# Five edits in a fused two-block transformer kernel: two earlier table loads, a later prefetch, a spreading stage that ends without waiting for its stores, and fewer score tiles beside it

## The reference, cut to what matters

```python
def rms_norm(x, g):
    y = xf * lax.rsqrt(jnp.mean(xf * xf, axis=-1, keepdims=True) + NORM_EPS)
    return (y * g).astype(x.dtype)

ml = (sc @ mod_w[i] + mod_b[i]).reshape(bsz, 1, N_MOD, d)      # modulation rows
hl = hl + ml[:, :, 5] * _peer_ffn(xl, pr_w_q[i], pr_keys[i], pr_u[i], pr_v[i])
hc = hc + mc[5] * _peer_ffn(xc, ...)                           # even layer only

# _peer_ffn: 8 heads choose 16 of 16384 rows for each token
a = jnp.einsum('nd,nhkd->nhk', xt, u[eidx])
w = gate * jax.nn.gelu(a, approximate=False)
return jnp.einsum('nhk,nhkd->nd', w, v[eidx])
```

## Time and profile before

| | us |
|---|---|
| median of 3 runs (3866.75 to 3868.51) | 3867.3 |
| the profiled execution's own time | 3863.82 |
| its span | 3862.0 |
| PE busy in the span | 3638.1 (94%) |
| PE weight loads | 3236.8 (84%) |
| DVE busy | 2690.2 (70%) |
| ACT busy | 1704.9 (44%) |
| POOL busy | 711.8 (18%) |

### The profile page before, as it was taken

How to read it: one execution, slowest core, us unless ns; L and a number is a source line. 1 busy time by engine, 2 the same in 40 slices (tenths; PEclk the granted TensorE clock), 3 DMA queues, 4 the chain that set the end, 5 groups by cost and what they waited for, 6 DMA issues and landing times. The chain is left out here.

```text
span 3862.0 us, 59455 instructions
## 1 busy us (share of the span) xinstructions
PE 3638.1 (94%) x22541; PEld 3236.8 (84%) x22541; DVE 2690.2 (70%) x5241; ACT 1704.9 (44%) x2738; POOL 711.8 (18%) x672
## 2 busy tenths in 40 slices
PE   8997999989999896999999999999988899999998
PEld 7895888878878776888899999999976888888887
DVE  5664666556665758887878868888566887777776
ACT  4454445445543544454222332223235554555554
POOL 0001000000010104554444313333010660000000
PEclk9998999999999998999999999999989999999999
DMA  6555655565542123346888868888421366556664
GB/s 250 190 203 213 246 189 214 186 231 201 186 143 103 47 77 120 121 167 259 304 316 302 317 222 312 306 307 313 176 94 61 132 239 234 214 212 213 213 223 164
DMA packets 166486, 793.72 MB, mean 206 GB/s; under 512 B 16608, under 2 KB 58176, under 8 KB 96992
## 3 DMA queue, kind: packets, MB, share of 16 engines
q1 hardware_dynamic: 120208, 603.88, 42.9%
q0 software_dynamic: 45744, 186.36, 13.5%
q10 hardware_dynamic: 288, 0.15, 0.0%
HBM read 743.04 MB, written 47.28 MB: 205 GB/s over the span
## 5 line engine op out<-in xcount | busy, mean ns | idle before, releaser
L247 DVE TENSOR_TENSOR units<-ring,units 128x1024 fp32r<-128x1024 f32 x857 | 1048.5, 1225 | 561.7 <-ACT units L240 558.2
L240 ACT ACTIVATE units<-ring 128x1024 fp32r<-128x1024 f32 x922 | 972.3, 1056 | 1009.0 <-PE ps L277 838.0
L276 PE MATMUL ps<-units,weighted 128*128 128x512 f32 x1280 | 501.3, 392 | 0.0
L275 PE MATMUL ps<-units,weighted 128*128 128x512 f32 x1280 | 499.4, 390 | 1.1 <-DVE units L247 1.1
L277 PE MATMUL ps<-units,weighted 128*128 128x512 f32 x1280 | 500.2, 391 | 0.0
L275 PE MATMUL ps<-wide_four,units 128*128 128x384 f32 (+1 forms) x1208 | 396.7, 328 | 8.7 <-PEq L3725 8.7
L277 PE MATMUL ps<-wide_four,units 128*128 128x384 f32 (+1 forms) x1208 | 394.9, 327 | 0.0
L276 PE MATMUL ps<-wide_four,units 128*128 128x384 f32 (+1 forms) x1208 | 394.4, 326 | 0.0
L277 PEld LDWEIGHTS ps<-units,weighted 128*128 128x128 f32 x1280 | 240.3, 188 | 51.2
L275 PEld LDWEIGHTS ps<-units,weighted 128*128 128x128 f32 x1280 | 240.9, 188 | 46.2 <-DVE units L247 1.5
L276 PEld LDWEIGHTS ps<-units,weighted 128*128 128x128 f32 x1280 | 240.7, 188 | 43.7
(11 more groups left out here) (592 smaller groups left out, 8141.1 us busy)
## 6 DMA issues: line engine op xcount, KB each, us to landing
ring<-in_stream SPq DMA_DIRECT2D x469, 1024.0 KB
quad_ring<-in_mod_w POOLq DMA_DIRECT2D x12, 4096.0 KB, 14.6
gates_dram<-gates_place SPq DMA_DIRECT2D x20, 2048.0 KB
gates_place<-gates_dram SPq DMA_DIRECT2D x16, 1536.0 KB
gates_place<-gates_dram SPq DMA_DIRECT2D x16, 1024.0 KB
gain_rows<-in_norm_gains SPq DMA_DIRECT2D x6, 512.0 KB, 4.4
peer_keys<-in_keys SPq DMA_DIRECT2D x3, 1024.0 KB, 6.3
ml_mask<-in_ml_mask SPq DMA_DIRECT2D x1, 2048.0 KB, 7.9
```

The lines of the kernel that those rows point to most:

```text
L240: act.activation(K.parts(n)[0], K.raw(n), ACT.Copy).then_inc(K.sig("hi_made").sem, units_to(K, n))
L247: dve.tensor_tensor(lo, K.raw(n), hi.bitcast(FP32), ALU.subtract).then_inc(K.sig("unit_split").sem, units_to(K, n))
L275: pe.matmul(out, w[0], x[0], start=start, stop=False)
L276: pe.matmul(out, w[0], x[1], start=False, stop=False)
```

## The change

The Sqrt table is asked for by a Sqrt of one element, in the opening ahead of the wait for x and in the odd layer's head ahead of the squares. There ACT now also copies the context tile out of PSUM, and DVE multiplies it by its row later, between the two norms. GpSimd's load of quad 0 comes after its other work and after 12 units are used. Five tiles are made beside each spreading (9 and 7 before), so 13 and 15 experts have their activations ahead, and the stream's order of units and the plan of picks follow. In spreading ACT evacuates everything before it splits the next two units, and the block ends without a wait for the stores. A part of each block is copied straight to where the first chunk of gates is read (SBUF to SBUF, beside the store), the first chunk is not loaded from DRAM, and the waits for the stores stand in the expert stage, on DVE ahead of the first gates and on SP ahead of chunk 1.

```diff
--- before.py
+++ after.py
@@ -61,8 +61,8 @@
 FFN_SLOTS = FT + FT // 2
 PEER_SLOTS = PEER_HEADS + KEYS
 
-AHEAD = 7, 7, 3
-AHEAD_BOTH = 5, 9, 3
+AHEAD = 7, 5, 3
+AHEAD_BOTH = 5, 5, 3
 
 
 TRIO = 3 * P
@@ -889,8 +889,11 @@
         self.picked_sum, self.loads = picked_sum, loads
 
     def scalar(self, act):
-        prepare_scalar(self.K, act, self.lat)
-        high_parts(self.K, act, self.lat, range(KD))
+        K, other = self.K, self.other
+        act.activation(other.y[:, 0, :], product(K, MT), ACT.Copy).then_inc(other.made.sem, 1)
+        act.activation(K.stat[:, 59:60], K.stat[:, 59:60], ACT.Sqrt)
+        prepare_scalar(K, act, self.lat)
+        high_parts(K, act, self.lat, range(KD))
 
     def between_scalar(self, act, c):
         if c == 0:
@@ -901,13 +904,12 @@
             high_parts(self.K, act, self.ctx, range(4 * c - 4, 4 * c))
 
     def vector(self, dve):
-        K, S, other = self.K, self.mine, self.other
+        K, S = self.K, self.mine
         dve.wait_ge(*S.loaded)
         for t in range(MT):
             dve.tensor_tensor(S.y[:, t, :], product(K, t), S.row, ALU.mult).then_inc(S.made.sem, 1)
             dve.wait_ge(*S.made.at(t + 1))
             dve.tensor_tensor(self.lat.src[:, t, :], S.res[t], S.y[:, t, :], ALU.add).then_inc(S.summed.sem, 1)
-        dve.tensor_tensor(other.y[:, 0, :], product(K, MT), other.row, ALU.mult).then_inc(other.made.sem, 1)
         prepare_vector(K, dve, self.lat)
         whole_columns(K, dve, self.lat, range(KD))
 
@@ -916,6 +918,8 @@
             K, S = self.K, self.other
             dve.wait_ge(*S.loaded)
             dve.tensor_tensor(S.y[:, 1, :], self.picked_sum, S.row, ALU.mult).then_inc(S.made.sem, 1)
+            dve.wait_ge(*S.made.at(1))
+            K.orders["dve"](dve, dve.tensor_tensor(S.y[:, 0, :], S.y[:, 0, :], S.row, ALU.mult))
             add_products(K, dve, S)
             prepare_vector(K, dve, self.ctx)
 
@@ -1645,11 +1649,12 @@
 
             @block.gpsimd
             def _(pool):
-                if opening is not None:
-                    load_quad(K, pool, 0)
                 entry_gpsimd(K, pool, entry)
                 if ahead is not None:
                     ahead.gpsimd(pool)
+                if opening is not None:
+                    pool.wait_ge(K.sig("unit_used").sem, 12)
+                    load_quad(K, pool, 0)
 
             @block.tensor
             def _(pe):
@@ -3790,18 +3796,18 @@
                         while taken < beside.count and beside.last_group(taken) < n - 1:
                             beside.scalar(act, taken)
                             taken += 1
+                while stores < groups // 2:
+                    store(stores)
+                    stores += 1
                 while taken < beside.count:
                     beside.scalar(act, taken)
                     taken += 1
                 for unit in beside.next_units():
                     split_hi(K, act, unit)
-                while stores < groups // 2:
-                    store(stores)
-                    stores += 1
     iota_made.past(1), iota_moved.past(1)
     by_act.past(groups // BUFFERS), by_pool.past(groups - groups // BUFFERS)
     compared.past(groups), spread.past(groups), stored.past(groups // 2)
-    beside.past(), keep.past()
+    beside.past()
 
 
 def u_unit(e, ahead):
@@ -3835,19 +3841,18 @@
     def before(self, act, t):
         g = t // SPAN
         if t % SPAN == 0 and g >= 2:
-            act.wait_ge(*self.moved[g % 2].at(16 * (g // 2)))
+            act.wait_ge(*self.moved[g % 2].at(32 * (g // 2)))
 
     def sync(self, sp, stored, tokens, also):
         for g in range(self.spans):
             also((g + 1) * SPAN)
             sp.wait_ge(*stored.at((g + 1) * SPAN // tokens))
+            sp.dma_start(self.chunks[0][:, g, :, :], self.blocks[g % 2][:, 0:CHUNK, :]).then_inc(self.moved[g % 2].sem, 16)
             sp.dma_start(self.dram[g], self.blocks[g % 2]).then_inc(self.moved[g % 2].sem, 16)
+
+    def wait_moved(self, eng):
         for n in range(2):
-            sp.wait_ge(*self.moved[n].at(16 * self.spans // 2))
-
-    def past(self):
-        for n in range(2):
-            self.moved[n].past(16 * self.spans // 2)
+            eng.wait_ge(*self.moved[n].at(16 * self.spans))
 
     def load(self, sp, c):
         sp.dma_start(self.chunks[c % 2].rearrange("p g e n -> p g (e n)"),
@@ -3855,16 +3860,18 @@
           .then_inc(self.moved[c % 2].sem, 16)
 
     def wait_loaded(self, eng, e):
-        if e % CHUNK == 0:
-            c = e // CHUNK
-            eng.wait_ge(*self.moved[c % 2].at(16 * (c // 2 + 1)))
+        c = e // CHUNK
+        if e == 0:
+            self.wait_moved(eng)
+        elif e % CHUNK == 0:
+            eng.wait_ge(*self.moved[c % 2].at(16 * self.spans + 16 * ((c + 1) // 2)))
 
     def gates(self, e):
         return self.chunks[e // CHUNK % 2][:, :, e % CHUNK, :]
 
-    def past_loads(self):
+    def past(self):
         for n in range(2):
-            self.moved[n].past(16 * KEYS // CHUNK // 2)
+            self.moved[n].past(16 * self.spans + 16 * (KEYS // CHUNK // 2 - 1 + n))
 
 
 GATHERS = 4
@@ -3952,8 +3959,9 @@
         with K.block() as block:
             @block.sync
             def _(sp):
-                for c in range(2):
-                    store.load(sp, c)
+                stream_weights(K, sp, u_unit(A, A) // 2)
+                store.wait_moved(sp)
+                store.load(sp, 1)
                 for c in range(2, KEYS // CHUNK):
                     done = CHUNK * (c - 1) - 1
                     stream_weights(K, sp, v_unit(done, A) // 2)
@@ -4104,7 +4112,7 @@
                     split_ahead(K, dve, split_lo, K.taken + KEYS)
     K.taken += KEYS
     early_taken.past(A - N), gelu_done.past(KEYS - A), weights_made.past(STEPS * KEYS)
-    store.past_loads()
+    store.past()
     if joint:
         lows_copied.past(KEYS - A), summed.past(KEYS - A)
     if picked is not None:
```

## The result

The changed kernel takes 3841.1 us, the median of 4 runs (3840.60 to 3849.32); the kernel before took 3867.8 in the same comparison (4 runs, 3866.75 to 3868.51). The ratio is 0.9937 [0.9924, 0.9949]: 26.7 us faster, where 3.7 were forecast, and outside the range. A second measurement of the same kernel gave 3842.9 (5 runs) against 3865.9 (24 runs), ratio 0.9938 [0.9925, 0.9952], 23.0 us.

The account below looks back on a forecast made before the run. PE was taken to bound the expert stretches, waiting for others only in the opening, the first spreading and the ends of spreading. Terms -2.8 - 5.4 + 0 - 8.6 + 22.3 - 8.2 - 1.2 + 0.2 = -3.7 gave median 3863.6 us, range 3856.5 to 3871.5.

Parts of the forecast that it names:

- my first term: First spreading, 9 to 5 tiles: DVE's waits for PE fall from 8.7 to 1.1 us; with restarts, 8.6 us gained.
- Opening, start: Opening, ahead of the first norm: two table loads leave ACT's path and x comes 0.4 earlier; 2.8 us gained.
- Stall: Opening, steps 1 to 4: ACT's wait for ring slot 3 and the slow PE behind it go; 5.4 us gained.
- Tiles' new place: Expert loops: six tiles move into the main part, four at 4.18 and two at 2.80 us; cost 22.3 us.
- Gaps: Ends of both spreadings: PE's wait falls from 8.7 and 8.8 to 4.6 us, 4.1 gained each, 8.2 in all.
- Clock after the gap: Behind both ends of spreading: PE loses 1.6 us to the slow clock, a gain of 0.6 each, 1.2 together.
- D: Rival: the gap is short enough for the fast clock to stay; 3860.4, or 3859.3 with x earlier; chance 0.15.
- Odd head: Odd layer's head: PE comes 1.1 us earlier and its unit 0.3 later; cost 0.2 us.
- B: Rival: the ring starves anyway in the opening, so the 5.4 us are lost; 3869.0; chance 0.12.
- C: Rival: the first spreading doesn't shrink, as a score piece still delays the compares; 3872.2, slower by 4.9; chance 0.10.
- F: Rival: the changed tiles do nothing because the pieces were free; excluded beforehand by 33 waits, given no chance.
- E: Rival: a table switch holds ACT longer than its record, so 3.8 us more would go; 3859.8; chance 0.08.

Follow-up runs that it names:

- The three single experiments: Kernel before with one part of the change each: the opening alone, ratio 0.9973; the tiles alone, 0.9987; the end of spreading alone, 0.9976.
- the two single edits: Kernel before with only the early Sqrt in the opening, 3864.84 us, and with only the later load of quad 0, 3859.50 us; one execution each.

## Why the prediction was wrong

**The step that failed** is the price of the spreadings. I divided a run of 118 compares without an idle row by 117, got 0.646 us, and took that for what DVE can do; from it came "The second stage, 7 to 5 tiles, has nothing to give but these 1.1: I take 0", and a first stage that could lose only its 8.7 us of shown waits with their restarts. DVE's own rate is 0.598: with three tiles all but a few steps at the start have it, and fewer tiles don't lower it. The 0.646 was a mean of two kinds of steps. The rows of the kernel before in narrow windows of the timeline, two pairs of compares out of that very run, then one pair of the even layer:

```profile
3110.55 1.41 DVE L3751 TENSOR_TENSOR hits<-ps,routes 128x512 f32<-128x512 f32 x2
3111.27 1.29 DVE L3751 TENSOR_TENSOR hits<-ps,routes 128x512 f32<-128x512 f32 x2
```

```profile
1680.84 1.47 DVE L3751 TENSOR_TENSOR hits<-ps,routes 128x512 f32<-128x512 f32 x2
```

A compare's record lasts 0.68 to 0.69 us, so two that follow at DVE's rate fill 1.28 or 1.29 together. The pair of 1.41 stands 0.72 apart, the pair of 1.47 0.78, the latter with 0.10 us of idle time between its two records. Neither is shown as a wait. Two things hide it: at full rate a record ends 0.68 - 0.598 = 0.08 us after the next compare could have begun, and a row of the timeline also takes in compares with a little idle time between them, 0.10 us here. What the late one waits for stands in the timeline of PE, same kernel:

```profile
3110.62 0.61 PE L3765 MATMUL ps<-hits 128*128 128x128 f32 x4
```

PE is through with a group at 3111.23, and the late compare starts at 3111.27. This holds throughout. In the even layer of the kernel before, 74 of 191 steps are over 0.62 us, in the odd one 49 of 127, and each of these compares starts 0.036 to 0.039 us after the end of PE's work on the group five before, the one whose buffer it takes (PE's ends are modelled, but the distance is always the same). Only 33 and 3 of them show a wait.

| time above 0.598 a step, us | even, before | even, change | odd, before | odd, change |
|---|---|---|---|---|
| late compares with a shown wait | 11.4 (33) | 1.6 (3) | 1.4 (3) | 0 |
| late compares without one | 7.5 (41) | 0.2 (2) | 5.4 (46) | 0.5 (3) |
| all other steps | 0.7 | 0.0 | 0.5 | 0.0 |
| together | 19.6 | 1.9 | 7.2 | 0.5 |

The difference is 17.7 us in the first stage and 6.7 in the second, as the spreadings measured. So the late compares without a shown wait, which I had at nothing, are 7.2 of the 9.1 us that my first term missed and 4.9 of the 6.7 of the second. The restarts, 0.08 us each and not 0.034, are 1.2 more in the first; the three shown waits with theirs are 1.4 in the second; 0.7 and 0.4 are steps of 0.61 in place of 0.60. Together 15.8 were missing, and the other terms take 0.5 of it back. The Trainium skill, Perfetto Trace Analysis, section Optimizing Scalar/DVE Operations, says that of the fixed time of each DVE instruction the half that acknowledges the write overlaps with the next one, so that the profiled latency is longer than the engine is busy; these rows agree in that, with 0.68 against 0.598.

The sign was to be had from the kernel before. Its first seven compares, where the first score piece of PE is still ahead (1660.23):

```profile
1654.37 4.28 DVE L3751 TENSOR_TENSOR hits<-ps,routes 128x512 f32<-128x512 f32 x7
```

(4.28 - 0.68) / 6 = 0.600 us, far below the 0.646 that I took for the rate. I had asked of such runs only whether a wait is shown.

With this the sum is: -7.0 for the opening, -17.7 and +16.9 for the even tiles, -6.7 and +5.6 for the odd ones, -5.1 and -5.2 for the two ends, +0.2 for the odd head, in all -19.0 us. The three single experiments give by their ratios -10.4, -5.0 and -9.3, together -24.7, each within some 4 us; the change as a whole -24 [-29, -19] in the second measurement. So the parts agree with the whole, as far as such intervals can tell: the -19.0 of the rows lies just inside that interval (and just outside the one of the first measurement, -29 to -20). The rest, 4 us against the second median and 8 against the first, is not settled. In the two profiled executions it is not one more stage of the change, since all stretches behind the first compare are accounted for to 2 us; the faster executions, which make the median, have no profile. In the first measurement the granted clock was 0.978 in the profiled execution and 0.980, 0.981 and 0.980 in the other three; 0.002 of 3841 us is, as an estimate, 8 us of full clock, and by 8 us they were shorter. In the second the order isn't that plain (3842.69 us at 0.978, 3843.57 at 0.980).

That the tiles cost 22.5 us, as forecast, and gave back 24.4 means that this edit by rows is worth 1.9 us. The gain of the change is that of the opening and of the two ends.

**The scatter** lies in code that the change doesn't touch, and goes at least partly with PE's clock. The kernel with the tiles alone is the kernel before up to the spreading, and reached its first compare at 1660.71 in place of 1654.37. Timeline of GpSimd, the kernel before and then the one with the tiles alone:

```profile
1105.91 2.43 POOL L571 TENSOR_TENSOR both_pair<-whole_columns,both_pair 128x256 fp32r<-128x256 f32 x2 [6.44 <-DVE whole_columns L564]
...
1451.44 0.14 POOL L3396 IOTA peer_iota<- 128x16 f32 x1 [133.35 <-POOLq L1345]
```

```profile
1105.70 2.43 POOL L571 TENSOR_TENSOR both_pair<-whole_columns,both_pair 128x256 fp32r<-128x256 f32 x2 [6.43 <-DVE whole_columns L564]
...
1457.59 0.14 POOL L3396 IOTA peer_iota<- 128x16 f32 x1 [133.37 <-POOLq L1345]
```

Level at 1106 us, they are 6.2 us apart at 1451. Two windows in between, the kernel before first, with the granted clock as the third number from the end:

```profile
1250.00:1300.00 50.00, 46.35 (x310) 39.52 (x310) 45.95 (x143) 26.46 (x72) 11.85 (x5) 0.93 0.17 64
1300.00:1350.00 50.00, 44.84 (x347) 42.07 (x346) 31.86 (x74) 27.98 (x57) 4.93 (x3) 0.97 0.13 44
```

```profile
1250.00:1300.00 50.00, 45.74 (x291) 39.31 (x292) 43.13 (x136) 23.11 (x64) 10.18 (x5) 0.89 0.13 46
1300.00:1350.00 50.00, 46.08 (x332) 43.05 (x331) 31.17 (x78) 26.52 (x59) 7.15 (x3) 0.91 0.17 62
```

Here PE has short waits, and where it loses the fast clock differs from execution to execution; 0.04 and 0.06 of 50 us are 2 and 3 us of full clock in these two windows alone. The kernel before ranged from 3862.75 to 3874.66 in 24 runs. But the clock is not all of it: the two profiled executions of the change, which reach their first compare 3.7 us apart, both spend 113 us at half clock up to there. That the difference between profiles and medians comes from the clock was not tried by itself.

**Point by point.** *Opening, start* (2.8): 2.4 up to the first split, 11.28 to 8.90, but 1.3 at step 1, because of the slow first products. Both table loads went as priced; x came at 6.19 and not 0.4 earlier; in the two single edits it came at 6.02 with the 4 MB beside it and at 6.07 without, so the 4 MB don't delay it. *Stall* (5.4): 5.4, steps 8.43 apart, and 5.5 with the later quad alone. *Later load* 0: right. *Tiles' new place* (22.3): 22.5. *Gaps* (4.6 each): 4.9 and 4.7. The chain is the one I named, but with a change of block of 0.60 at its end, and with ACT's split begun only after the last evacuation, 0.73 behind PE's end. *Clock after the gap* (0.6 each): the even stretch to the first product became 5.1 shorter, of which 3.8 is the gap, so 1.3. In the 20 us behind the gap the granted clock rose from 0.89 to 0.91; slow matmuls (0.53 us in place of 0.34) last until 1780.56 in the change. D, that the fast clock would stay, is wrong. *Odd head* (+0.2): right in its sum. *Stores* 0 and chunk 0 from SBUF, 0: right, no wait for gates. *B* is refuted by the evenly spaced steps, *C* by 116.8 us (a piece does delay a compare, but with five tiles hardly ever), *F* stayed excluded. *E*, the dearer table switch: after the new table load, 1.70 to 2.98, the small Sqrt stands at 2.99, so again nothing follows the load; the drain of the Trainium skill, ScalarE: Activation LUTs, section What ACT_TABLE_LOAD costs, is not seen in this trace either.

The range ended at 3856.5 because its good ends were those of terms as I had priced them. The first spreading was allowed 9.7 us at most and gave 17.7; the second was put at 0 with no range of its own and gave 6.7.

## What to carry to other kernels

An unbroken run of instructions in the profile doesn't show that its engine sets the pace. Look at the spacing of neighbouring instructions inside the run, not at the mean of the run, and compare it with the same instruction where nothing else holds it up; the smallest spacing is the engine's rate, and every longer step has a cause to be looked for. Work that is put beside a stage is free only up to the corner where the other engine takes over; here the corner lay at 5.4 tiles, and each one beyond it cost 5.0 us in place of the 4.2 that it saved. Where two branches meet, here the norm and the first ring slot, an edit that shortens only one can be worth nothing (here the table load alone), so such edits must be priced together.

## What the runs showed of the hardware

DVE's back-to-back compares of 128x512 (0.68 us alone) came 0.598 us apart at best, and a compare that came 0.12 to 0.18 us late showed no wait in the timeline.

With 4 MB in flight from GpSimd's queue at the start, SP's issue of one small table took 5.99 us, and 1.65 without. It goes with the 4 MB and not with the table load: 5.88 us with the early table load alone, 1.68 with the later quad alone. What holds it up isn't shown. The row in the kernel before and then in the changed kernel, second measurement, timeline of SP:

```profile
5.57 5.99 SPq L1785 DMA_DIRECT2D decay<-in_ret_log_decay  x1
```

```profile
5.53 1.65 SPq L1790 DMA_DIRECT2D decay<-in_ret_log_decay  x1
```

The first norm didn't wait for it: with the early table load alone the first Square starts at 6.02, in the middle of that issue.
